# Where a recurrent tile's output projection stands among the norms, who squares and who sums, and a projection split in two

## The reference, cut to what matters

```
h = x                                            # (tokens, 1024)
for layer in (0, 1):
    xn = rmsnorm(h, norm_mix)
    h += lru_mixer(xn)   if layer == 0 else gmlp_mixer(xn)
    g, u = split(rmsnorm(h, norm_ffn) @ w_up)    # 3072 + 3072
    h += (gelu(causal_conv3(g) + b) * u) @ w_down
    h += sigmoid(rmsnorm(h, norm_ple) @ w_gate) * (p @ w_proj)
out = rmsnorm(h, norm_final)

lru_mixer:  gate, xb = split(xn @ w_in); xc = causal_conv4(xb)
            r, i = sigmoids of block-diagonal products of xc
            hs_t = a_t*hs_{t-1} + sqrt(1-a_t^2)*(i_t*xc_t), a = sigmoid(lam)^(8r)
            y = (gelu(gate) * hs) @ w_out
gmlp_mixer: u, v = split(gelu(xn @ w_in)); v = layernorm(v)
            s = masked 128x128 matrix per group over the tokens of a chunk, applied to v, + bias
            y = (u * s) @ w_out
```

## Time and profile before

| | |
|---|---|
| runs | 1772.71 us median of 3 (1771.36 to 1954.47) |
| profiled execution | 1774.49 us; span on its slowest core, core 1, 1772.9 us |
| spans of the eight cores | 1766.2 to 1772.9 us |
| PE busy | 1657.3 us (93%), 10844 matmuls |
| DVE, ACT, POOL busy | 1266.0 (71%), 951.9 (54%), 642.3 us (36%) |
| PE idle | 107.3 us before its matmuls |

### The profile page before, as it was taken

How to read it: one execution, slowest core, us unless ns; L and a number is a source line. 1 busy time by engine, 2 the same in 40 slices (tenths; PEclk the granted TensorE clock), 3 DMA queues, 4 the chain that set the end, 5 groups by cost and what they waited for, 6 DMA issues and landing times.

```text
span 1772.9 us, 35646 instructions; the slowest of 8 cores (1766.2 to 1772.9 us)
## 1 busy us (share of the span) xinstructions
PE 1657.3 (93%) x10844; PEld 1051.1 (59%) x10844; DVE 1266.0 (71%) x2596; ACT 951.9 (54%) x1935; POOL 642.3 (36%) x1103
## 2 busy tenths in 40 slices
PE   5799999799999999999999999899999999999994
PEld 2456656466666666666644555566666666666653
DVE  4566657997766677676757877797676767777766
ACT  3777788654434444456655453854444444447664
POOL 1333345522111111136866654811111111125672
PEclk9899999899999999999999999999999999999997
DMA  7630030045030212110192000044130303030004
GB/s 140 132 103 1 1 68 10 1 95 105 5 69 16 57 29 45 26 36 1 28 181 41 1 1 8 10 72 72 26 72 2 72 1 72 1 60 1 34 11 164
DMA packets 21818, 82.96 MB, mean 47 GB/s; under 512 B 1792, under 2 KB 12864, under 8 KB 15744
## 3 DMA queue, kind: packets, MB, share of 16 engines
q0 software_dynamic: 8224, 59.16, 18.7%
q1 hardware_dynamic: 12432, 20.32, 3.3%
q10 hardware_dynamic: 976, 1.21, 0.3%
HBM read 129.81 MB, written 10.03 MB: 79 GB/s over the span
## 4 chain that ended last, share of the span: by engine, by line
PE 74%; DVE 8%; issue 6%; ACT 5%; POOL 5%; DMA 1%; ACTq 0%; DVEq 0%; POOLq 0%
PE PS L582 74%; DVE SB L566 5%; POOL SB L541 4%; ACT SB L530 2%; DVE SB L541 2%; ACT L530 1%; ACT PS L530 1%; DMA SB<-cst 1%; DVE SB L557 1%; DMA SB<-lru_w_x 1%; ACT SB L571 0%; POOL SB L557 0%; POOL SB L573 0%; POOL SB L555 0%; DVE SB L1318 0%
## 5 line engine op out<-in xcount | busy, mean ns | idle before, releaser
L582 PE MATMUL PS<-SB 128*128 128x352 bf16 (+5 forms) x10844 | 1657.3, 314 | 107.3 <-ACT SB L530 33.1
L582 PEld LDWEIGHTS PS<-SB 128*128 128x128 bf16 x10844 | 1051.1, 99 | 713.3 <-issue 157.0
L566 DVE SCALAR_TENSOR_TENSOR SB<-SB 128x352 f32<-128x352 f32 (+1 forms) x720 | 401.2, 576 | 227.6 <-ACT SB L571 200.7
L541 POOL TENSOR_TENSOR SB<-SB 128x352 f32<-128x352 f32 (+11 forms) x448 | 430.3, 975 | 271.5 <-PE PS L582 88.2
L541 DVE TENSOR_TENSOR SB<-SB,PS 128x352 f32<-128x352 f32 (+3 forms) x960 | 459.0, 514 | 79.2 <-PE PS L582 64.6
L530 ACT ACTIVATE SB<-PS,SB 128x352 f32<-128x352 f32 (+1 forms) x432 | 258.4, 614 | 366.7 <-PE PS L582 354.8
L530 ACT ACTIVATE SB<-SB 128x352 f32<-128x352 f32 (+5 forms) x670 | 318.4, 503 | 241.8 <-DVE SB L566 152.4
L573 POOL COPY SB<-SB 128x2 f32<-128x2 f32 (+2 forms) x472 | 152.1, 327 | 676.4 <-ACT SB L571 579.8
L566 DVE SCALAR_TENSOR_TENSOR SB<-SB,PS 128x352 bf16<-128x352 f32 (+6 forms) x448 | 222.4, 547 | 115.6 <-ACT PS L530 72.1
L571 ACT ACTIVATE SB<-PS 128x352 f32<-128x352 f32 (+6 forms) x408 | 160.0, 408 | 22.6 <-PE PS L582 15.6
L530 ACT ACT_TABLE_LOAD x104 | 133.4, 1283 | 69.4 <-PE PS L582 52.5
(11 more groups left out here) (27 smaller groups left out, 49.4 us busy)
## 6 DMA issues: line engine op xcount, KB each, us to landing
SB<-ffn_w_up POOLq DMA_DIRECT2D x24, 1024.0 KB, 10.1
SB<-ffn_w_down POOLq DMA_DIRECT2D x12, 1024.0 KB, 8.4
SB<-xT SPq DMA_DIRECT2D x10, 704.0 KB, 9.8
yT<-SB SPq DMA_DIRECT2D x10, 704.0 KB, 3.4
SB<-ple_w_gate POOLq DMA_DIRECT2D x2, 2048.0 KB, 14.4
SB<-gm_w_in POOLq DMA_DIRECT2D x2, 2048.0 KB, 15.8
SB<-pT POOLq DMA_DIRECT2D x2, 1056.0 KB, 14.4
SB<-lru_w_x_in POOLq DMA_DIRECT2D x4, 512.0 KB, 11.6
```

Of the source, the lines that this page charges most:

```text
L541: emit(eng, lambda e: e.tensor_tensor(out=out.ap, in0=a.ap, in1=b.ap, op=op), R=[a, b], W=[out], cost=c)
L566: emit("dve", lambda e: e.scalar_tensor_tensor(out=out.ap, in0=a.ap, scalar=sa, in1=b.ap, op0=op0, op1=op1), R=rr, W=[out], cost=c)
L582: emit("pe", lambda e: e.matmul(ps.ap, lhsT=lhsT.ap, rhs=rhs.ap, start=start, stop=stop), R=[lhsT, rhs], W=[ps], cost=max(0.05, 0.000427 * ...
```

## The change

It does four things. In `bg`, `out` moves behind xn4. The norms xn2 to xn5 take the second form, with all eight squares on POOL. In layer 0's slice 0, for tiles 0 to 2, tap 1 becomes an ACT Identity (scaled) into a new buffer `tap0` and a POOL add into `A`; `tap0` is a single buffer for all twelve. In the gMLP, W(4) runs its groups 0 to 3 at its old place and groups 4 to 7 after S(5), ahead of W(5); so that S(5) can write while W(4) still reads, tile 5's gated product has a buffer of its own, `ggate5`, in the place of the layernorm's gain and bias.

```
+        ggate5 = T(mem, [KC, 320], BF16, off=lng.off)
+        tap0 = T(mem, [TN], F32, off=gg[1][4].off)

-        bg.append(("xn2", xn_norm("nf0", 2)))
+        bg.append(("xn2", xn_norm("nf0", 2, None, "pool", False)))
         bg.append(("tail", lru_tail()))
-        bg.append(("xn3", xn_norm("nf0", 3)))
+        bg.append(("xn3", xn_norm("nf0", 3, None, "pool", False)))
+        bg.append(("xn4", xn_norm("nf0", 4, None, "pool", False)))
         bg.append(("out", lru_out()))
-        bg.append(("xn4", xn_norm("nf0", 4)))
-        bg.append(("xn5", xn_norm("nf0", 5)))
+        bg.append(("xn5", xn_norm("nf0", 5, None, "pool", False)))

-                for j in (1, 0):
+                shared = l == 0 and s == 0 and ti < 3
+                if shared:
+                    act(tap0.all(), gb.v((1, 1 + npr)), AF.Identity, scale=vcol(fw, 24 + cg))
+                    tt(A.v((0, npr)), A.v((0, npr)), tap0.all(), ALU.add, eng="pool")
+                for j in (0,) if shared else (1, 0):
                     stt(A.v((0, npr)), gb.v((j, j + npr)), vcol(fw, j * 24 + cg), A.v((0, npr)), ALU.mult, ALU.add)

-                tt(ggate.v(g, (0, n)), uv, sv, ALU.mult, eng="dve" if g % 2 or g == 6 else "pool")
+                tt((ggate5 if ti == 5 else ggate).v(g, (0, n)), uv, sv, ALU.mult, eng="dve" if g % 2 or g == 6 else "pool")

-        def g_W(ti):
+        def g_W(ti, ms=range(KC)):
-            for m in range(KC):
+            for m in ms:
...
-                g_W(ti)
+                g_W(ti, range(KC) if ti < 4 else range(4))
             else:
                 bg.append(("xn0", xn_norm("nf1", 0, (gsq.off, 2))))
                 g_S(ti)
                 bg.append(("xn1", xn_norm("nf1", 1)))
-                g_W(ti)
+                g_W(4, range(4, KC))
+                g_W(5)
```

More of the change, by code:

```diff
@@ L1374, in g_S @@
                 tick()
-        def g_W(ti):
+        def g_W(ti, ms=range(KC)):
             c0, npr, ns = GTILES[ti]
             n = npr + ns
-            for m in range(KC):
+            for m in ms:
                 ps = B7(n)
                 for k in range(KC):
-                    mm(ps, gw_o.v(k, (m * 128, (m + 1) * 128)), ggate.v(k, (0, n)), k == 0, k == KC - 1)
+                    mm(ps, gw_o.v(k, (m * 128, (m + 1) * 128)), (ggate5 if ti == 5 else ggate).v(k, (0, n)), k == 0, k == KC - 1)
                 tt(hv(m, c0, n), hv(m, c0, n), ps, ALU.add)
```

## The result

| | before | after |
|---|---|---|
| median of the runs, us | 1772.63 (5 runs, 1771.36 to 1954.47) | 1759.55 (5 runs, 1757.71 to 1761.08) |
| ratio after/before | | 0.9929, 95% interval 0.9913 to 0.9945 |
| profiled execution, us | 1774.49 | 1761.08 |
| PE idle before its matmuls, us | 107.3 | 98.0 |
| layer 0's first FFN slice, us | 111.6 | 104.5 |

The account below looks back on a forecast made before the run. PE bounds the steady FFN; the change acts in two stretches where PE idles, the first put down to DVE. Gains of 5 (2 + 3.9 - 1) and 2.5 us make 7.5, 1774.49 to 1767.0, less 1.8 for the median: 1765, range 1750 to 1777.

Parts of the forecast that it names:

- Projection later, 2 us: First FFN slice: scans come due about a tile later, DVE takes evictions and taps first; 2 us gained from DVE's idle time.
- Norms, counted at nothing: First FFN slice: 15.7 us of squares and 11.6 us of waits leave ACT, which does not end the stretch; gain 0.
- Tap, 3.9 less 1: First FFN slice: DVE's 6.2 us of relief minus 2.3 of contention, less 1 us for the longer way to Gelu.
- The term for contention, 2.3 us: First FFN slice: 8.2 us more POOL work slows DVE's stt by 0.43 per us, scaled 23/35; bounds 0 and 8.2.
- DVE's relief, 6.2 less 1: First FFN slice: 12 stt off DVE save at least 6.2 us; 1 us lost to the longer ACT, POOL, DVE way.
- The rule on the two SBUF sides: First FFN slice: by exclusive access POOL's added 8.2 us come off DVE in full, giving -1 us instead of 5.
- xn5 in time, slice 1's load hidden: End of first slice: xn5 ready in 12 to 13 us against tile 4's 14.3; 28.7 us of matmuls cover the 10 us load.
- POOL's tensor work +8.2: First FFN slice: 11.4 us of adds plus 23.7 of squares minus 26.9 of sums make POOL's tensor work grow 8.2 us.
- The end of the gMLP, 2.5 us: Split W(4): W(5) starts 1.6 us earlier, 1.4 from the filled wait and clock; 2.5 of 3.0 us kept, bounds 0 and 7.
- The tap chain becomes the wait, slower: Rival, tiles 0 to 2: single tap0 makes ACT wait for POOL's adds; 6 to 15 us slower, about 1780, chance 0.13.
- Both holes close: Rival, both stretches: a better order removes idle and low clock, 12 us in the first and 7 in the second; 1754, chance 0.20.
- POOL takes back what it relieves: Rival: first stretch gains nothing through DVE's contention or POOL's late queue, second gains 2 to 3 us; 1770, chance 0.18.

Follow-up runs that it names:

- the idle adds: Changed kernel with both taps on DVE, the 12 ACT operations and 12 POOL adds still issued into a buffer nobody reads: 1764.47 us, ratio 0.9952.
- the squares in turn: Changed kernel with each norm's eight squares dealt out in turn, even blocks on ACT, odd blocks on POOL: 1761.15 us, ratio 0.9928.

## Why the prediction was right, and where not

The total came out in the range, which is 27 us wide around an effect of 13. It lies as far from the forecast of 1765 as from the rival of 1754. The sum's 7.5 us were 12.5, and both stretches were undersized. That the first slice came as near as 5 for 7.1 is luck: the norms stood in it at nothing and the tap at a gain of 2.9, and in the order projection, tap, norms they are worth 2.0 gained, 7.0 lost and 12.2 gained.

The first slice by its parts, all eight combinations, us:

| | tap on DVE | tap on ACT and POOL |
|---|---|---|
| old norms, old place | 111.6 | 116.9 |
| old norms, projection later | 109.7 | 116.7 |
| new norms, old place | 107.0 | 106.7 |
| new norms, projection later | 106.2 | 104.5 |

(The split doesn't touch this stretch: 111.4 with it alone. The kernels of the corners "new norms, old place, tap shared", "new norms, later, tap on DVE" and "old norms, later, tap shared" hold it.)

- **Projection later, 2 us: held.** 2.0 alone, 2.2 beside all else, 0.8 and 0.2 in the two other pairs (the last two are no more than the cores differ by). The scans do become later by it: alone it moves all eight past 340 us. In the changed kernel only three are there (346.72, 349.97 and 350.89); three run before 313 and two more at 326.95 and 331.04, spread over 55 us, where they stood within 14. It is the new norms that bring three forward: with them alone these run at 301.45, 305.29 and 308.54. I had not seen that.
- **Norms, counted at nothing: this step failed.** "ACT is not what ends the stretch, so I count none of it" took the engine of PE's last wait, DVE, for the cause. DVE's instructions were themselves late, or slow, through what stood before them. Taking the sums and squares away is worth 4.6 us alone, 3.5 beside the later projection, and 10.2 and 12.2 beside the tap. Beside the tap the record shows one thing that they held, the tap's adds: DVE waits for these 7.0 and 7.8 us with the old norms, 3.8 in the changed kernel. That is 4 of the 12.2 us; how the rest comes about is not shown. ACT's 11.6 us of waits for the sums, the row that the prediction quoted, can be little of it: they go with the projection's move alone, for 2 us. What the 4.6 and 3.5 us are made of stays open too, apart from the 2.9 us by which `stt` became shorter. The 12.2 have two parts, as the run with the squares on ACT shows: 7.7 us from the end of POOL's chained sums, 4.5 from the squares' move from ACT to POOL. The 4.2 us of new matmuls were paid: the slice has 28 more, and is shorter all the same.
- **Tap, 3.9 less 1: wrong as a term of its own.** It costs 5.2 us with the old norms and 7.0 with the projection moved too; with the new ones it gains 0.3 and 1.7. It is no term that can be added. The term for contention, 2.3 us, is what the idle adds cost; but it had been worked out for 8.2 us more of POOL work, and the runs had 11.2. By `stt` time the price is 0.28 us per us, not 0.43; I had divided by the 22.3 us of one group of POOL's adds, and POOL had 43.78 us of work in that window. DVE's relief, 6.2 less 1, came to 4.0.
- **The rule on the two SBUF sides.** The wrong step here was mine: I let all of POOL's added time come off DVE, which gave -1 for the stretch (and 8 to 11 us in the expectation for the idle adds), and took the rows, being less, to lie between that and nothing. The 11.2 us of adds cost 3.1 us of `stt` time and 2.3 us of the slice, and the stretch gained 7. By the Trainium skill, page "SBUF — State Buffer", section "SBUF: two separate sides", a DVE instruction with two SBUF inputs and a GpSimd instruction that reads SBUF exclude each other for the whole instruction. The traces agree: each `stt` that began well inside a POOL add, product or square ended 0.38 us after it. They don't agree with a price of POOL's full time, since most `stt` did not begin inside one (13 of 36 did with the idle adds).
- **xn5 in time, slice 1's load hidden: held** (the wait of 0.18 us; no wait of PE at slice 1).
- **POOL's tensor work +8.2: held.** All of it in the program went from 430.3 us in 448 operations to 437.8 in 464, which is 32 and 12 more and 28 fewer.
- **The end of the gMLP, 2.5 us: mechanism right, too small.** 4.4 us with all parts, and the term that was too small is the clock: PE's waits went from 6.7 us to between 5.8 and 6.6, and 3.4 to 10.2 us at the low clock became 3.4 or none. W(5)'s stretch, from its first matmul to layer 1's, went from 13.9 to 10.9 us: 1.2 by less waiting (0.92 and 0.84 in place of 0.59 and 2.42), the other 1.8 because no low clock is left in it; I had 1.4 for both. What comes ahead of it is 1.0 us shorter by the median of the differences on each core, not 1.6. (The prediction took 1119.31 us for the start of W(5). That is its seventh matmul; the first stands at 1114.94, and the waits of 0.59 and 2.42 us are inside the first group, which reads the eight products one after the other.) I also took off 0.5 as given back in layer 1's first slice, and that came out 1.0 shorter. There was no wait near 4 us before the fourth u group, but one of 1.93 before the fifth: the first three adds of W(4) run directly behind the LayerNorm's last operation, and the planner put the fourth u group and the first spatial groups ahead of the wait.

The rivals. *The tap chain becomes the wait, slower* had its mechanism in the wrong place: not the single `tap0` (ACT waits 1.6 us for POOL in the kernel with the tap, the later projection and the old norms, DVE 7.8), but POOL's queue, where the tap's add stands behind another generator's chain of sums. By itself it happens, at 5 us, and the new norms are what removes it; I named that as the argument against it and then gave the norms no credit. *Both holes close* was half true: PE's idle time fell to 5.7 us in the first stretch, and in the second hardly, but the clock's dip closed for the most part. *POOL takes back what it relieves* fell with the 2.3 us.

Open: why the order with two tap buffers is worse by 4.7 us, where the norms' gain comes from beyond the waits named above, and what ends the 9.1 us still lost in the first slice (104.5 less 640 matmuls of 0.149). The expectation for the squares in turn speaks of 4.4 us of waits; that came from a wrong count of 672 matmuls, and PE's idle time there is 5.7 us.

## What to carry to other kernels

An engine that ends PE's waits need not be the one to relieve: look what its late instructions waited for, and price a part that removes a chain of dependent operations by the waits behind the chain, not by the busy time of its engine. A wait on record is no price yet: ACT's 12.1 us of waits for POOL fell to 0.7 by another part, and the slice became 2 us shorter. Work that is handed to a third engine joins that engine's queue; if a chain stands there in which each operation reads the last, the handed work is late by what is left of the chain (3.4 us here, in a wait of 5.65) though the engine has room. Test such parts in pairs, since the sign of one (tap, +5.2 to -1.7 us) can depend on another.

## What the hardware showed that I had not expected

- Two long waits cost more here than nearly the same time in small pieces. In the gMLP PE waited 6.7 us before and 5.8 to 6.6 after, yet 4.4 us were won: after the waits of 3.70 and 2.42 us the granted clock was 0.50 and 0.61; with waits of at most 1.93 us it stayed at 1.00 on core 1 and fell once, for 3.4 us, on core 2. Small waits are no safeguard: with the cut after two groups, waits of 1.93, 1.73 and 0.67 us are followed by a window at 0.62.
- A two-input `stt` that begins inside a POOL add, product or square ends 0.38 us after it, in every such case from 300 to 395 us of nine of the kernels (85 of 85 with more than 0.25 us of the POOL operation left). Its time grows from 0.58 to as much as 1.29 us.
- Adds on POOL that each read the last run one per 1.13 us, 0.93 for the add and 0.20 between, in the timeline of the kernel with the old norms. Independent operations stand without that gap: six squares in 5.34 us, 0.89 each, beside DVE's work.
- A buffer more made the kernel slower by 4.7 us in one slice. Each change of a dependency re-orders queues that are laid out by a planner, and the effect of that can be larger than that of the dependency.
